# RG-LRU gates as two 64-row tiles of TensorE, with the second chunk's gates moved into the third chunk's projection

## The reference, cut to what matters

```python
hn = rms_norm(x, norm_mix_pre)                       # x: 1024 tokens x 1024
lru_x, lru_gate, q, k, v = split(hn @ w_in)          # 512 each
xc = causal_conv4(lru_x) + conv_b
xb = xc.reshape(B, T, 8, 64)                         # 8 blocks of 64 channels
r = sigmoid(einsum("bthi,hij->bthj", xb, w_gate_a) + b_gate_a)
i = sigmoid(einsum("bthi,hij->bthj", xb, w_gate_x) + b_gate_x)
log_a = -8 * r * softplus(-lru_lambda)
a, b = exp(log_a), sqrt(-expm1(2 * log_a)) * (i * xc)
y_lru = linear_scan(a, b) * gelu(lru_gate)
# then differential attention on q, k, v; output projection; MLP of 4096
```

## Time and profile before

| what | value |
|---|---|
| median of 3 runs | 1155.19 us (1154.11 to 1155.8) |
| the profiled execution | 1152.76 us, span 1151.0 us |
| mean granted TensorE clock | 0.996 of full |
| TensorE matmul busy | 1122.8 us, 98% of the span |
| VectorE busy | 785.3 us, 68% |
| ScalarE busy | 399.2 us, 35% |
| chain that ended last | TensorE 89%, VectorE 5%, transfers 2% |

### The profile page before, as it was taken

The page is one execution under the profiler, slowest core; times in us unless marked ns, Lnnn a source line. Parts: engine busy times, 40 slices in busy tenths (PEclk is TensorE's granted clock), DMA queues, the critical chain, the costliest instruction groups (busy, mean ns, idle before and its releaser), DMA issues.

```text
span 1151.0 us, 14008 instructions
## 1 busy us (share of the span) xinstructions
PE 1122.8 (98%) x5110; PEld 908.4 (79%) x5110; DVE 785.3 (68%) x1127; ACT 399.2 (35%) x728; POOL 52.7 (5%) x94
## 2 busy tenths in 40 slices
PE   7999999999989999999999999999999999999996
PEld 6888887777756788878888888888888888888885
DVE  6666765756577546888867667766766666766768
ACT  7433933545567326642212112212221211211222
POOL 0300001000121110000000000000000000000010
PEclk9999999999999999999999999999999999999998
DMA  6111323111010456111121011110211102111062
GB/s 229 56 37 36 136 84 89 58 37 38 21 35 19 148 182 200 73 37 74 37 73 36 36 73 36 45 64 36 73 36 41 69 36 73 36 36 73 37 234 113
DMA packets 23397, 83.11 MB, mean 72 GB/s; under 512 B 3088, under 2 KB 3216, under 8 KB 23232
## 3 DMA queue, kind: packets, MB, share of 16 engines
q1 hardware_dynamic: 17424, 62.92, 15.3%
q0 software_dynamic: 5648, 19.60, 5.0%
q10 hardware_dynamic: 288, 0.09, 0.0%
HBM read 70.02 MB, written 8.39 MB: 68 GB/s over the span
## 4 chain that ended last, share of the span: by engine, by line
PE 89%; DVE 5%; DMA 2%; ACT 1%; issue 1%; SPq 0%; POOL 0%; DVEq 0%; ACTq 0%
PE pair L352 27%; PE pair L354 27%; PE pair L353 27%; PE pair L725 3%; PE pair L760 2%; DMA raw<-weights 2%; PE pair L742 1%; PE pair L728 1%; DVE y_gain L2087 1%; PE pair L574 1%; DVE yacc L2072 1%; DMA q_rot<-q_sb 1%; DVE h_sb L2101 1%; DVE negmax L1657 0%; DVE wl L1478 0%
## 5 line engine op out<-in xcount | busy, mean ns | idle before, releaser
L354 PE MATMUL pair<-wdh,xl 128*128 128x512 f32 x480 | 186.7, 389 | 0.0
L352 PE MATMUL pair<-wdh,xh 128*128 128x512 f32 x480 | 186.7, 389 | 0.0
L353 PE MATMUL pair<-wdl,xh 128*128 128x512 f32 x480 | 186.7, 389 | 0.0
L1883 DVE TENSOR_TENSOR yacc<-yacc,pair 128x1024 f32<-128x1024 f32 x104 | 127.0, 1221 | 80.2 <-PE pair L354 80.2
L1378 ACT ACTIVATE up_h<-raw 128x384 fp32r<-128x384 f32 x56 | 27.4, 513 | 226.9 <-DMA raw<-weights 226.9
L353 PEld LDWEIGHTS pair<-wdl,xh 128*128 128x128 f32 x480 | 90.1, 188 | 18.7
L352 PEld LDWEIGHTS pair<-wdh,xh 128*128 128x128 f32 x480 | 90.1, 188 | 18.7
L354 PEld LDWEIGHTS pair<-wdh,xl 128*128 128x128 f32 x480 | 90.1, 188 | 18.7
L352 PE MATMUL pair<-xh,wh 128*128 128x512 f32 x256 | 102.2, 399 | 1.0 <-DVE xl L1501 1.0
L354 PE MATMUL pair<-xh,wl 128*128 128x512 f32 x256 | 99.9, 390 | 0.0
L353 PE MATMUL pair<-xl,wh 128*128 128x512 f32 x256 | 99.7, 389 | 0.0
(11 more groups left out here) (305 smaller groups left out, 2099.1 us busy)
## 6 DMA issues: line engine op xcount, KB each, us to landing
raw<-weights SPq DMA_DIRECT2D x74, 512.0 KB, 3.3
wd_f<-weights SPq DMA_DIRECT2D x28, 512.0 KB, 3.6
x_sb<-x SPq DMA_DIRECT2D x8, 512.0 KB, 7.7
q_rot<-q_sb POOLq DMA_DIRECT2D x32, 128.0 KB, 2.7
out<-h_sb POOLq DMA_DIRECT2D x8, 512.0 KB, 3.5
h_sb<-out POOLq DMA_DIRECT2D x8, 512.0 KB, 11.2
out<-h_sb SPq DMA_DIRECT2D x7, 512.0 KB, 2.6
x_a<-x POOLq DMA_DIRECT2D x4, 512.0 KB, 6.8
```

The source lines that it names most:

```text
L352: pe.matmul(o, a_hi, b_hi, start=first, stop=False)
L353: pe.matmul(o, a_hi, b_lo, start=False, stop=False)
L354: return pe.matmul(o, a_lo, b_hi, start=False, stop=last)
L1883: dve.tensor_tensor(y, y, pair[2 + t % 2][:, :], ALU.add).then_inc(y_added, 1)
```

## The change

The gate weights of a chunk are laid out as one 128 x 128 tile instead of two padded ones: rows 0 to 63 hold wa and wx of the chunk's first block side by side, rows 64 to 127 wx and wa of its second block. `gate_products` multiplies rows 0 to 63 into `pair[2]` and rows 64 to 127 into `pair[3]`, alternating between the two row halves: 12 matmuls over 512 columns as before, each of 64 rows. `pair[2]` then holds r of the first block on partitions 0 to 63 and i of it on 64 to 127, `pair[3]` i of the second block on 0 to 63 and r of it on 64 to 127. ScalarE therefore does four sigmoids over 64 partitions in place of two over 128. `gwh` and `gwl` have 128 columns in place of 256. gates(1) moves from before chunk 2 to between the two halves of chunk 2's u piece; TensorE's loop over chunks 2 and 3 is written out for that. The conversion of P_VA+2 moves on ScalarE from behind the first Exp and Square to ahead of the last tanh, and on VectorE from behind the first `bsq` to ahead of it.

```diff
             def gate_products(c):
                 pe.wait_ge(xc_lo, c + 1)
-                for g in range(2):
-                    for hf in range(2):
-                        tok = slice(HALF * hf, HALF * hf + HALF)
-                        mm = mm3(pe, pair[2 + g][:, tok], gwh[:, g, :], gwl[:, g, :], xch[:, tok],
-                                 xcl[:, tok], True, True)
-                    mm.then_inc(gates_done, 1)
+                for hf in range(2):
+                    tok = slice(HALF * hf, HALF * hf + HALF)
+                    for n, (w, u) in enumerate(((gwh, xch), (gwh, xcl), (gwl, xch))):
+                        for g, rows in enumerate((slice(0, 64), slice(64, P))):
+                            mm = pe.matmul(pair[2 + g][:, tok], w[rows, :], u[rows, tok], start=n == 0, stop=n == 2)
+                            if n == 2:
+                                mm.then_inc(gates_done, 1)
...
-            gate_products(1)
-            with pe.Fori(2, LC) as c:
+            for c in range(2, LC):
                 for s in range(2):
                     pe.wait_ge(w_lo, 2 * c + s + 1)
-                    for mm in feature_piece(s, pair[s], xh, xl):
-                        pass
+                    for hf, mm in enumerate(feature_piece(s, pair[s], xh, xl)):
+                        if c == 2 and s == 0 and hf == 0:
+                            gate_products(1)
                     mm.then_inc(piece_used, 1)
                 gate_products(c)
...
-                act.wait_ge(gates_done, 2 * c + 1)
-                act.activation(dec[:, c, :], pair[2][:, :], ACT.Sigmoid,
-                               bias=cols[:, bass.ds(c + C_BA, 1)]).then_inc(sig_done, 1)
-                act.wait_ge(gates_done, 2 * c + 2)
+                act.wait_ge(gates_done, 4 * c + 4)
+                act.activation(dec[0:64, c, :], pair[2][0:64, :], ACT.Sigmoid,
+                               bias=cols[0:64, bass.ds(c + C_BA, 1)]).then_inc(sig_done, 1)
+                act.activation(dec[64:P, c, :], pair[3][64:P, :], ACT.Sigmoid,
+                               bias=cols[64:P, bass.ds(c + C_BA, 1)]).then_inc(sig_done, 1)
                 act.wait_ge(ix_done, c)
-                act.activation(lru_a[:, :], pair[3][:, :], ACT.Sigmoid,
-                               bias=cols[:, bass.ds(c + C_BX, 1)]).then_inc(sig_done, 1)
+                act.activation(lru_a[0:64, :], pair[2][64:P, :], ACT.Sigmoid,
+                               bias=cols[0:64, bass.ds(c + C_BX, 1)]).then_inc(sig_done, 1)
+                act.activation(lru_a[64:P, :], pair[3][0:64, :], ACT.Sigmoid,
+                               bias=cols[64:P, bass.ds(c + C_BX, 1)]).then_inc(sig_done, 1)
                 act.wait_ge(gelu_in, c + 1)
                 act.activation(lru_g[:, :], lru_g[:, :], ACT.Sigmoid, scale=GELU_S).then_inc(gelu_sig, 1)
-                act.wait_ge(sig_done, 2 * c + 2)
+                if c == LC - 1:
+                    hi_early(P_VA + 2)
+                act.wait_ge(sig_done, 4 * c + 4)
...
-                if c < 2:
-                    hi_early(P_VA + 2 + c)
+                if c == 1:
+                    hi_early(P_VA + 3)
...
-                dve.tensor_tensor(gwl[:, :, :], gw_raw[:, c, :, :], gwh[:, :, :].bitcast(F32), ALU.subtract)
+                dve.tensor_tensor(gwl[:, :], gw_raw[:, c, :], gwh[:, :].bitcast(F32), ALU.subtract)
...
-                dve.wait_ge(sig_done, 2 * c + 2)
+                dve.wait_ge(sig_done, 4 * c + 4)
...
+            lo_early(P_VA + 2)
             for c in range(LC):
                 dve.wait_ge(decay_sq, c + 1)
                 dve.wait_ge(tanh_done, LC)
                 dve.scalar_tensor_tensor(u_t[:, c, :], (lru_a, lru_g)[c % 2][:, :], 1.0, u_t[:, c, :], ALU.add,
                                          ALU.mult).then_inc(bsq_done, 1)
-                if c < 2:
-                    lo_early(P_VA + 2 + c)
+                if c == 1:
+                    lo_early(P_VA + 3)
```

More of the change, by code:

```diff
@@ L116, in build @@
         lru_g = sb("lru_g", [P, T], F32, at_s + 12 * KB)
-        gwh = sb("gwh", [P, 2, P], F32R, at_s + 16 * KB)
-        gwl = sb("gwl", [P, 2, P], F32R, at_s + 17 * KB)
+        gwh = sb("gwh", [P, P], F32R, at_s + 16 * KB)
+        gwl = sb("gwl", [P, P], F32R, at_s + 17 * KB)
         cos_t = sb("cos_t", [P, 2, T], F32, at_s)
@@ L189, in build @@
         hrstd = small("hrstd", [P, 32])
-        gw_raw = sb("gw_raw", [P, LC, 2, P], F32, at_v)
+        gw_raw = sb("gw_raw", [P, LC, P], F32, at_v)
         lam_raw = sb("lam_raw", [P, 4, 64], F32, at_s + 18 * KB)
@@ L511, in _ @@
             pool.wait_ge(squares_v, 2)
-            pool.dma_start(gw_raw[:, :, :, :], gate_weights).then_inc(gates_loaded, 16)
+            pool.dma_start(gw_raw[:, :, :], gate_weights).then_inc(gates_loaded, 16)
             links = [0]
@@ L536, in _ @@
             nc.gpsimd.tensor_scalar(spl[:, 1, :], acc, -LRU_C, None, ALU.mult).then_inc(spl_ready, 1)
-            pool.wait_ge(gates_done, 2 * LC)
+            pool.wait_ge(gates_done, 4 * LC)
             pool.dma_start(cos_t[:, :, :], rope).then_inc(rope_loaded, 16)
@@ L672, in _ @@
                 else:
-                    pe.wait_ge(sig_done, 2 * LC)
+                    pe.wait_ge(sig_done, 4 * LC)
                 for j in range(N_V):
@@ L1111, in _ @@
                 act.wait_ge(conv_done, c + 1)
-                act.activation(gwh[:, :, :], gw_raw[:, c, :, :], ACT.Copy)
+                act.activation(gwh[:, :], gw_raw[:, c, :], ACT.Copy)
                 act.activation(xch[:, :], xc_t[:, c, :], ACT.Copy).then_inc(xc_hi, 1)
@@ L2150, in lay_out_gates @@
 def lay_out_gates(wa, wx):
[L2152 to L2156, removed]
+    g = np.empty((P, LC, P), np.float32)
+    for c in range(LC):
+        g[0:64, c, 0:64], g[0:64, c, 64:P] = wa[2 * c], wx[2 * c]
+        g[64:P, c, 0:64], g[64:P, c, 64:P] = wx[2 * c + 1], wa[2 * c + 1]
     return g
```

## The result

The changed kernel is slower. Its median is 1156.59 us (1155.18 to 1158.55, 20 runs), beside 1153.79 us (1151.72 to 1155.8, 20 runs) for the kernel before. The ratio is 1.0030, 95% interval 1.0023 to 1.0036, so +3.5 us, between +2.6 and +4.2. The forecast was +0.8 us with a range of 1153.6 to 1158.6. The time lies in the range, but the likeliest case, "no measurable change" (0.0 to +1.8, with 2.3 us as the least that can be told), did not happen: the whole interval lies above it. The profiled execution has a span of 1153.4 us and a time of 1155.18.

What follows compares the result with a forecast made beforehand. TensorE alone was taken to set the pace from 50 to 180 us. Sigmoids +2.0 and lateness +0.15, less 1.3 us slack, gave about +0.8 us on the 1155.19 median: 1156.0 us, range 1153.6 to 1158.6.

Steps and rivals of the forecast that it cites:

- no measurable change: Whole kernel: the forecast case, 0.0 to +1.8 us, chance 0.65; 0.68 for "same" when drawn wider.
- rival (c): Gate products on TensorE: row tiles do not overlap, 2.9 us for a chunk's gates, time 1158.6 us; chance 0.08.
- Start of chunk 2: TensorE stalls 3.3 us for VectorE's low part and starts chunk 2 at 67.2, before at 67.70.
- P_VA+3: Value piece whose low part is ready at 132.7; TensorE wants it at 132.05 and waits 0.65 us.
- Waits at each later value piece: VectorE's round takes 5.7 us, TensorE's piece 5.45, so once TensorE waits it waits in all that follow.
- VectorE's chain behind the last sigmoids: After chunk 3: TensorE waits for it, so P_QK starts at 161.15 instead of 160.28, 0.8 to 0.9 us later.
- the price of a sigmoid over 64 partitions: ScalarE: each costs a full 1.0 us, so +2.0 us per chunk; bounds 0 to +2.0.
- the saving of the gates: TensorE: a chunk's gates take 1.6 us instead of 2.72; four chunks save 4 x 1.12 = 4.5 us.
- the +0.85 of P_QK: Start of P_QK: +2.0 for sigmoids and +0.15 of lateness, less 1.3 us slack; 0.8 to 0.9 us later.
- rival (d): Pause before chunk 2: the clock falls in the stall, +1.6 to +5.45 us, time 1157.6 to 1161.5; chance 0.13.
- only the longer pause at the end: Earlier trace: clock kept full level in a 2 us pause, fell about 1144.4 after the last matmul at 1141.15.
- costs about as much as it frees: Move of gates(1): left in place they would wait for `xcl`, which ends 1.1 us ahead of the low part.

Runs made afterwards that it cites:

- the pause filled: Changed kernel with 12 unused spare products in TensorE's pause before chunk 2: ratio 1.0019 to the kernel before, P_QK +1.80 us.
- the first four experiments: Changed kernel with spare products before chunk 2 (1.0019) or two sigmoids (0.9985); kernel before with four sigmoids (1.0034); row tiles in chunks 1, 2 only (0.9985).
- a kernel with spare products: Row tiles in chunks 1 and 2 only, plus 8 unused products in TensorE's pause ahead of the first scores: 0.9974, again 0.9965, to the kernel before.
- the second four experiments: Changed kernel with gates(1) back (1.0014) or conversion back (1.0049); row tiles in chunks 1 to 3 (0.9996); chunks 1, 2 with scores' pause filled (0.9974).

## Why the prediction was right in its course and wrong in its likeliest case

**Right, by the step.** Two products of 64 rows do run at once, and rival (c) is out. Start of chunk 2: 67.2 foreseen, 67.13 measured, with a pause of 2.98 us ended by VectorE's `wl`. The place is right, the closeness is luck: up to the last sigmoid of chunk 0 the price was +2.40 in place of +2.0, and two gains that the sum did not have took it back, the first sigmoid 0.32 earlier (49.52 against 49.84, behind shorter gates(0)) and VectorE's `u_t` 2.28 behind its product in place of 2.44. P_VA+3: a wait of 0.65 foreseen, 0.89 measured. Waits at each later value piece: in the profile after, the first products of pieces stand at 146.48, 152.19, 157.90 and 163.61, 5.71 us apart, VectorE's round. That VectorE's chain behind the last sigmoids sets the start of P_QK is so, and with it the place of the conversion matters, as the experiment that puts it back shows.

**The first terms that were off: the price of a sigmoid over 64 partitions, and the saving of the gates.** For a sigmoid I took 1.0 us from start to start, from the earlier trace rows; it is 1.13. Two more of them and the slower pace of all four make 4.54 - 2.0 = +2.5 us a chunk in place of +2.0. Behind chunk 3 that is 0.5 us more than foreseen. For the gates I took 1.6 us, a saving of 1.12; the 1.59 measured over the same distance looks like a hit, but the saving is 0.92, since the change to 64 rows and back also slows the products on either side. That is most of the 0.4 us by which the values start late (116.12 with the pause filled, 115.7 foreseen); TensorE's wait for `xcl` of chunk 2 was 0.06 us of it. Together 0.9, which makes the +0.85 of P_QK the +1.80 that was measured with the pause filled. The bounds that I gave for the sigmoids, 0 to +2.0, did not hold the true value: I left no room above "a full one each".

**The second: rival (d) came true on top of the forecast.** I gave a fallen clock a chance of 0.13 and priced it at +1.6 or more. It fell at 68.7, eight to nine products were 0.2 us longer each, and P_QK was 1.66 us later than with the pause filled. It costs what I had as its lower price. How often it fell there is open. It was seen in the profile after and not in the one with the conversion back, behind the same 2.98 us. The mean clocks speak for "often": of the 20 runs of the changed kernel none had over 0.994, while of the 28 runs of the kernel before that stood beside the first four experiments 13 had 0.995 or more, and half the clock for 3.4 us (the 0.57 from 68 to 72 above) is 0.0015 of a span, about the size of that shift. With the pause filled 3 of 11 had 0.995 or more.

The step of the prediction that failed is its reading of the earlier trace rows. It says that in the trace before "only the longer pause at the end" brought the clock down. That is not so. At about 328.6 us the clock of that same trace fell behind waits of 1.74 and 0.92 us with some matmuls between them:

```profile
327.07 0.59 PE L725 MATMUL pair<-xc_t 64*128 64x128 f32 x4 [1.74 <-DVE xc_t L1633]
...
328.95 1.97 PE L742 MATMUL pair<-ident,probs 128*128 128x128 f32 x8 [0.92 <-DVE probs L1651]
```

Windows of PE:

```profile
326.00:328.00 2.00, 0.93 (x6) 1.00 0.00 0
328.00:330.00 2.00, 1.08 (x6) 0.66 0.00 0
330.00:332.00 2.00, 2.00 (x9) 0.50 0.00 0
```

A pause of some 3 us called for a greater chance than 0.13 beside that row. In later profiles the clock fell behind the single pause of 1.5 to 2.0 us ahead of the scores six times. The Trainium skill ("TensorE: Matmul & The Clock Gate", Why this matters for your kernels) had warned of such a pause. The profile after agrees with it, 0.57 behind 2.98 us; the profile with the conversion back does not, 1.00 behind 2.98 us, and the six falls ahead of the scores came behind shorter pauses than it warns of.

Sigmoids and gates (0.95) and the clock (1.66) make up the difference: 0.85 + 0.95 + 1.66 = 3.46 us at P_QK. By the end of the profiled executions it is 2.4 us, by the medians 2.8 and by the ratio 3.5. Part of it is lost again to small waits that come out shorter (ahead of the scores 1.6 us in place of 2.0). The rest I did not follow.

**A claim that fell.** I wrote that the move of gates(1) "costs about as much as it frees". It is a loss by itself: with gates(1) in its old place, and the clock kept in both, P_QK comes 1.45 us earlier. The prediction's own numbers said so. Done inside the pause, the gates would have ended at 67.7 and delayed chunk 2 by 0.5 us (measured 0.36: 67.49 against 67.13), whereas behind it they are 1.6 us of path (1.8 with the change of rows and back). They also cut the pause from 2.98 to 1.83 us, and in that profile the clock was kept; that the shorter pause kept it is not shown, since it was also kept once behind 2.98.

**Where the expected gain went.** TensorE's work did shrink, by 4 x 0.92 = 3.7 us in place of the 4.5 foreseen. gates(0)'s part fell into the pause. gates(3)'s fell into VectorE's chain. The parts of gates(1) and gates(2) are real, 1.9 us, and are kept by the kernel that uses row tiles in these two chunks alone (P_QK -1.88).

## What to carry to other kernels

Faster products pay only where the engine that feeds or drains them has slack in that very round; of four equal rounds here the two in the middle gained and the first and last lost, so apply such a change round by round. When work is taken out of a pause, price the pause: what stands in it is nearly free. When a trace is asked whether pauses bring the clock down, go through the granted clock of the whole kernel and not of two chosen pauses. And a product on TensorE that is cheaper by leaving results at half height hands its cost to ScalarE, at more than full price for each instruction.

## What the runs showed of the hardware

- A sigmoid over 64 partitions and 1024 columns out of PSUM takes 1.13 us from start to start, one over 128 partitions 1.0. Shown durations are alike (1.11 and 1.10); what goes is the overlap with the instruction behind it, whether that is over 64 or 128 partitions. It is so with and without a change of partitions. Why was not tried.
- Two products of 64 rows and 512 columns in fp32r run together at full pace: a pair stands 0.23 us from the next (74.75, 74.99, 75.22 in the profile after, as for one product of 128 rows). The change to 64 rows and the one back to 128 each stretch two distances by some 0.1 us, the one into the new form (74.10 to 74.42, 75.68 to 76.00) and the one behind it (74.42 to 74.75, 76.00 to 76.34), 0.4 us in all.
- TensorE's clock fell to 1.2 GHz behind single pauses of 1.5 to 3.3 us, and held in others of 1.6 to 2.1 us and in one of 2.98. It also fell, in twelve of thirteen profiles, from 326 us on, at a wait of 1.7 us and a shorter one with matmuls between them. The length of a pause alone does not decide it here. The fall at 68 us (3.4 us at the lower level) cost 1.66 us, and the one at 327 us in a kernel with spare products (6.8 us) cost 2.58 us against a profile without it. Falls are a good part of the spread between runs of the same kernel: of the 29 runs of the kernel before beside the second four experiments, 9 with a mean granted clock of 0.996 averaged 1152.3 us and 10 with 0.994 averaged 1154.0.
